# The opening of a two-block transformer on one core: modulation rows by column tiles, mean square by token, two lru chunks worked in pairs of blocks

## The reference, cut to what matters

```python
mod = (c @ w_ada + b_ada)[:, None, :]            # c: 1 x 1024, w_ada: 1024 x 6144
sh_m, sc_m, g_m, sh_f, sc_f, g_f = jnp.split(mod, 6, axis=-1)
h = rms_norm(x) * (1 + sc_m) + sh_m              # x: 512 tokens x 1024
proj = h @ w_in
x_lru, q_down, kv_down, k_rope, gate_a, gate_b = jnp.split(proj, IN_SPLIT_POINTS, axis=-1)
y_a = rg_lru(causal_depthwise_conv(x_lru, conv_w, conv_b), positions, ...)
```

## Time and profile before

| | before |
|---|---|
| median of three runs | 3159.71 us |
| the profiled execution's own time | 3160.7 us |
| its span | 3159.0 us |
| TensorE (PE) busy | 2889.7 us, 91% |
| VectorE (DVE) busy | 1243.8 us, 39% |
| ScalarE (ACT) busy | 748.3 us, 24% |
| mean granted TensorE clock | 0.957 |

### The profile page before, as it was taken

The page is one execution under the profiler, slowest core; times in us unless marked ns, Lnnn a source line. Parts: engine busy times, 40 slices in busy tenths (PEclk is TensorE's granted clock), DMA queues, the critical chain, the costliest instruction groups (busy, mean ns, idle before and its releaser), DMA issues.

```text
span 3159.0 us, 36442 instructions
## 1 busy us (share of the span) xinstructions
PE 2889.7 (91%) x13284; PEld 1776.6 (56%) x13284; DVE 1243.8 (39%) x2119; ACT 748.3 (24%) x1068; POOL 111.2 (4%) x171
## 2 busy tenths in 40 slices
PE   6997899999999899999998979999998999998984
PEld 5775578887778667788776763333332333332221
DVE  6883656765484454334266531111111111111113
ACT  3633432122373334222232320000000000000001
POOL 0020000000000000000010000000000000000001
PEclk7999999999999999999988979999999999999997
DMA  7264136664314022242322059594699979979995
GB/s 234 80 215 132 56 109 183 193 190 124 107 56 118 14 67 67 78 116 77 90 68 85 14 200 383 202 380 150 239 408 410 395 304 408 410 301 410 410 410 197
DMA packets 392991, 638.66 MB, mean 202 GB/s; under 512 B 28400, under 2 KB 278384, under 8 KB 392896
## 3 DMA queue, kind: packets, MB, share of 16 engines
q1 hardware_dynamic: 374784, 590.76, 52.3%
q0 software_dynamic: 9376, 31.14, 2.8%
q10 hardware_dynamic: 8736, 15.47, 1.4%
HBM read 610.77 MB, written 26.54 MB: 202 GB/s over the span
## 4 chain that ended last, share of the span: by engine, by line
PE 72%; DVE 7%; SPq 7%; DMA 7%; ACT 5%; issue 2%; POOL 0%; ACTq 0%; DVEq 0%; another core or an unknown queue 0%
PE bank L2274 24%; PE bank L189 13%; PE bank L191 12%; PE bank L190 12%; SPq L2164 5%; DMA ring<-w_down 4%; DMA ring<-w_gate 2%; PE bank L196 1%; PE bank L2279 1%; PE bank L899 1%; PE bank L900 1%; SPq L295 1%; PE bank L2266 1%; PE bank L940 1%; DVE WLO L162 1%
## 5 line engine op out<-in xcount | busy, mean ns | idle before, releaser
L2274 PE MATMUL bank<-ring,xT 128*64 128x512 f32 x3200 | 717.7, 595 | 43.8 <-DMA ring<-w_gate 21.6
L189 PE MATMUL bank<-HH,WHI 128*128 128x512 f32 x1360 | 551.5, 406 | 34.4 <-DVE HL L573 24.8
L190 PE MATMUL bank<-HL,WHI 128*128 128x512 f32 x1360 | 534.9, 393 | 0.0
L191 PE MATMUL bank<-HH,WLO 128*128 128x512 f32 x1360 | 534.5, 393 | 0.0
L2274 PEld LDWEIGHTS bank<-ring,xT 128*64 128x64 f32 x3200 | 220.1, 137 | 490.9 <-issue 384.6
L2274 PE MATMUL bank<-ring,hT 128*64 128x512 f32 x1600 | 360.0, 595 | 27.5 <-DMA ring<-w_down 25.8
L162 DVE TENSOR_TENSOR WLO<-RAW,WHI 128x2048 fp32r<-128x2048 f32 (+1 forms) x133 | 283.1, 2128 | 134.5 <-ACT WHI L154 134.4
L189 PEld LDWEIGHTS bank<-HH,WHI 128*128 128x128 f32 x1360 | 258.5, 190 | 108.4 <-DVE HL L573 20.4
L154 ACT ACTIVATE WHI<-RAW 128x2048 fp32r<-128x2048 f32 (+1 forms) x133 | 236.6, 1779 | 238.3 <-PE bank L191 177.5
L190 PEld LDWEIGHTS bank<-HL,WHI 128*128 128x128 f32 x1360 | 259.6, 191 | 54.0 <-issue 3.7
L191 PEld LDWEIGHTS bank<-HH,WLO 128*128 128x128 f32 x1360 | 258.8, 190 | 55.2
(11 more groups left out here) (397 smaller groups left out, 2920.5 us busy)
## 6 DMA issues: line engine op xcount, KB each, us to landing
ring<-w_gate SPq DMA_DIRECT2D x128, 1024.0 KB, 11.7
ring<-w_up SPq DMA_DIRECT2D x128, 1024.0 KB, 14.3
ring<-w_down SPq DMA_DIRECT2D x128, 1024.0 KB, 15.9
RAW<-w_ffn_in SPq DMA_DIRECT2D x88, 512.0 KB, 5.2
RAW<-w_ada SPq DMA_DIRECT2D x40, 1024.0 KB, 5.3
RAW<-w_in SPq DMA_DIRECT2D x37, 1024.0 KB, 5.6
RAW<-w_ffn_out SPq DMA_DIRECT2D x32, 704.0 KB, 4.7
expert_results<-ysb ACTq DMA_DIRECT2D x102, 128.0 KB, 5.5
```

Of the source, the lines that this page charges most:

```text
L189: pe.matmul(out, lhi, rhi, start=start, stop=False)
L190: pe.matmul(out, lhi, rlo, start=False, stop=False)
L191: return pe.matmul(out, llo, rhi, start=False, stop=stop)
L2274: ins = pe.matmul(out[halves(h), :], xT[:, k % 4, halves(k // 4)], m["ring"][:, c, at:at + 512], start=False, stop=k == KD - 1)
```

## The change

Loads: positions go before x, x comes in four parts by token tile, and mask comes last. The eight w_ada pieces go into four slots `pairs`; a pair p is column piece p (shift) and piece p + 4 (scale), and is loaded among the w_in chunks: pair 0, w_in 0 and 1, pairs 1 to 3, w_in 2 and 3. Pair 2 waits for rows(0), pair 3 for rows(1), the lru gate weights for rows(3).

Mean square: ScalarE squares each token tile of x as loaded, with an accumulator (one number per token), takes the root of 128x4; VectorE's reciprocal is of 128x4; TensorE spreads it with `root(0)`. The Sin moves behind the last HH.

Modulation: `rows(p)` multiplies with c, repeated 32 times, as the stationary operand and the weights as the moving one, 16 matmuls of 256 columns, in four tiles of 32 columns of the array; VectorE copies the rows to acc, `turned(p)` turns and adds them into columns of bank 6 (4 matmuls). Blocks 2p and 2p + 1 can then be normalized. `first_products(p)` does those two blocks for both first lru chunks (four banks). gates(0) stands between the halves of lru 2, gates(1) after it.

```diff
 def layer_loads(sp, L, m, W):
+    def pair(p):
+        if p >= 2:
+            sp.wait_ge(*sg.event("rows", p - 2))
+        for c in range(2):
+            i = p + 4 * c
+            sp.dma_start(m["pairs"][:, 2 * (p % 2) + c, :].rearrange("p (k n) -> p k n", k=KD),
+                         w_ada[:, :, i * 256:(i + 1) * 256]).then_inc(*sg.inc(f"pair_in{p}", also=[("pair", p)], n=16))
...
+        if not L.prev and n in PAIRS_BEFORE:
+            for p in PAIRS_BEFORE[n]:
+                pair(p)
...
-                sp.wait_ge(*start.event("ada_done"))
+                sp.wait_ge(*sg.event("rows", 3))
@@ layer_act
+    def opening():
+        for k in range(KD):
+            if k % 2 == 0:
+                act.wait_ge(*sg.event("pair_out", k // 2))
+            act.wait_ge(*sg.event("dve_h", ("n", 0, k)))
+            if k >= 2:
+                act.wait_ge(*sg.event("hl", (0, k - 2)))
...
+            act.activation(m["nh"][:, k % 2, :], source, ACT.Identity, **h)
+            act.activation(HH[:, k, :], source, ACT.Identity, **h).then_inc(*sg.inc("act_hi", ("h", 0, k)))
+            if k == 1:
+                feed(1)
+        act.wait_ge(*start.event("st_ang"))
+        act.activation(m["T"][:], m["ang"][:], ACT.Sin)
@@ layer_dve, opening()
+        scaled(0)
+        for p in range(4):
+            c = 2 * p
+            v.wait_ge(*sg.event("rows", p))
...
+            v.tensor_copy(m["acc"][:, p % 2, :], b[5 if p % 2 else 7][:, 0:256]).then_inc(*sg.inc("dve_out", ("rows_sb", p), also=[("rows_sb", p)]))
+            v.wait_ge(*sg.event("pair_col", p))
+            v.tensor_tensor(mod[:, c:c + 2], b[6][:, c:c + 2], vec[:, V_BADA + c:V_BADA + c + 2], ALU.add)
...
+            if p < 3:
+                scaled(p + 1)
+            if p == 0:
+                feed(1)
+            rest(p)
@@ layer_pe
+    def rows(p):
+        pe.wait_ge(*sg.event("pair", p))
...
+        for k in range(KD):
+            for c in range(2):
+                q = 32 * (2 * c + k % 2)
+                ins = pe.matmul(out[q:q + 32, 0:256], m["c"][:, k:k + 1].broadcast_to([P, 32]),
+                                m["pairs"][:, 2 * (p % 2) + c, k * 256:(k + 1) * 256], start=k < 2, stop=k >= KD - 2)
...
+    def first_products(p):
+        for g in range(4):
+            hi, lo = weights(g // 2)
...
+            for k in (2 * p, 2 * p + 1):
...
+                ins = split3(pe, b[g][:], hi[:, c:c + P], lo[:, c:c + P], HH[:, k, :], HL[:, k, :], k == 0, k == KD - 1)
...
+        pe.wait_ge(*start.event("st_eva", 4))
+        root(0)
...
+        rows(0)
+        turned(0)
+        for p in range(4):
+            if p < 3:
+                rows(p + 1)
+                turned(p + 1)
+            first_products(p)
+        dense("lru", 2, between=lambda: gates(0))
+        gates(1)
+        dense("lru", 3)
+        gates(2)
@@ start_program
-        engine.dma_start(m["x0"][:], W["x"][0].rearrange("(t p) d -> p t d", p=P)).then_inc(*sg.inc("st_x", n=16))
+        for t in range(NT):
+            sp.dma_start(m["x0"][:, t, :], W["x"][0, t * P:(t + 1) * P, :]).then_inc(*sg.inc(f"st_x{t}", n=16))
...
-            engine.activation(m["sq"][:, k % 2, :], m["X"][:, k, :], ACT.Square).then_inc(*sg.inc("st_sq", k))
+            act.activation(m["sq"][:].rearrange("p a n -> p (a n)"), m["x0"][:, t, :], ACT.Square, accum_out=m["rc"][:, t:t + 1]).then_inc(*sg.inc("st_sq"))
```

More of the change, by code:

```diff
@@ L328, in norm @@
     def norm(t, eps):
[L330 to L337, removed]
+        act.wait_ge(*(sg.event("stat", t) if t else L.prev.sg.event("stat", 2)))
+        act.activation(m["rc"][:], b[4][:, 0:NT], ACT.Sqrt, bias=K[:, eps:eps + 1], scale=1.0 / D).then_inc(*sg.inc("act_root", t))
         scale, shift = (8, 0) if t == 0 else (32, 24)
@@ L555, in norm @@
         v.wait_ge(*sg.event("act_root", t))
[L556 to L563, removed]
+        root = b[4]
+        v.reciprocal(m["rc"][:], m["rc"][:]).then_inc(*sg.inc("dve_out", ("rc", t), also=[("rc", t)]))
+        v.wait_ge(*sg.event("spread", t))
         for k in range(KD + 1):
@@ L581, in layer_dve @@
         modulate(b[6], 0, 48, ("ada_out", 0), ("ada_out", 1))
+        norm(0)
     else:
-        v.wait_ge(*start.event("ada_done"))
-        modulate(b[6], 0, 16, ("ada_out", 0))
-    norm(0)
+        opening()
     sm, hb = m["sm"], m["hb"]
@@ L829, in dense @@
         for j in range(2):
+            if j and between:
+                between()
             out = bank(g + j)
@@ L851, in layer_pe @@
     if L.prev:
         root(0)
[L853 to L856, removed]
+        for i in range(4):
+            dense("lru", i, norm=None if i else 0)
+            if i:
+                gates(i - 1)
+    else:
+        pe.wait_ge(*start.event("st_eva", 4))
+        root(0)
+        pe.wait_ge(*start.event("st_c"))
+        pe.wait_ge(*start.event("st_eva", 6))
+        rows(0)
[9 more added lines that the diff above has]
+        gates(2)
@@ L966, in layer_pe @@
     stat(2, (KD - 2, KD - 1))
[L969 to L970 removed]
+START_SIGNALS = "st_x0 st_x1 st_x2 st_x3 st_k st_mask st_c st_pos st_dve st_xt st_ev st_eva st_sq st_root st_ang"
 def start_program(engine, who, sg, m, b, W):
@@ L1075 @@
+    if who == "pe":
+        pe = engine
+        pe.wait_ge(*sg.event("st_k"))
+        for t in range(NT):
+            pe.wait_ge(*sg.event(f"st_x{t}"))
+            for k in (4, 1, 0, 3, 2, 5, 6, 7):
+                ins = pe.transpose(b[k][:, t * P:(t + 1) * P], m["x0"][:, t, k * P:(k + 1) * P], K[:, K_ID:K_ID + P])
+                if t == NT - 1:
+                    ins.then_inc(*sg.inc("st_xt", k))
 TWO_PI = (6.28125, 0.0019350051879882812, 3.019915981956753e-07)
@@ L1240, in _ @@
         def _(pe):
-            phases_of(pe, "pe", lambda e, L, after: layer_pe(e, L, m, b), lambda e, n: moe_pe(e, moe, m, b, n))
+            phases_of(pe, "pe", lambda e, L, after: layer_pe(e, L, start, m, b), lambda e, n: moe_pe(e, moe, m, b, n))
         @block.gpsimd
```

165 lines of the change are left out of this document (81 added, 84 removed).

## The result

The changed kernel takes **3144.15 us** (median of 7 runs, 3138.20 to 3145.52) and the kernel before 3161.39 us (7 runs, 3153.96 to 3164.47). The ratio is 0.995, with a 95% interval of 0.9939 to 0.9960: 17.2 us faster by the medians. The forecast was 3146 us. The profiled execution of after has 3138.2 us, span 3136.4, and is the fastest of its seven; the one of before had 3160.7 and 3159.0.

The account below looks back on a forecast made before the run. The opening's chain through TensorE's statistics and matrix-vector products, then the lru tails, was taken to bound the kernel. T0 13.8 us earlier gave 3146.9 from 3160.7, less 1.0 above the median: 3146 us, range 3138 to 3157.

Parts of the forecast that it names:

- T0: Start of the first lru tail on ScalarE, after gates(0); forecast 82.6 us, 13.8 earlier than 96.40, the end moving equally.
- Pair cost, 2.3 us: Sixteen modulation matmuls of a pair on four 32-wide column tiles: 2.3 us at full clock, 4.5 at half.
- rows(0) 4.5 and turned(0) at half clock: First modulation pair on TensorE at half clock: rows(0) from 18.5 to 23.0, copy and turned(0) to 25.4 us.
- Products start at 38.6: First products on TensorE start at 38.6 us instead of 63.0, after VectorE's WLO, HL and copy for pair 1.
- Clock: TensorE's clock in the first product phase: 4 us at half, making it 38.6 to 45.9; other three phases 5.5 each.
- Sin not hidden, 1.9 us: Sin moved ahead of ScalarE's exp load adds 1.28 us table load and 0.6, since VectorE's log1p waits for exp.
- xc sets this and not TensorE: VectorE's xc steps end at 79.1 and set T0; TensorE waits 2.8 us for WLO 2, losing that gain.
- Rival 1: Column tiles share only in part: a pair 3.9 us at full clock, T0 86.7 to 88.6, 3150 to 3153; chance 0.15.
- Rival 2: Column tiles do not overlap: a pair 7.2 or 14.4 us, T0 about 102, 3166 us, nothing gained; chance 0.10.
- Rival 4: TensorE's clock stays at half through the four product phases, 10.3 us each: T0 110.7, 3174 us; chance 0.05.
- Rival 3: A just-covered link between 82.6 and 267 us becomes the wait, such as TensorE's clock: 3152 to 3158; chance 0.08.
- Rival 5: All better: full clock from 18.5 us and pairs of 1.8 us, T0 75.5, 3139 us; chance 0.07.

Follow-up runs that it names:

- e1: Changed kernel with the 16 matmuls of a modulation pair issued one column tile after the other; 3151.56 us, ratio to before 0.9973.
- e4: Changed kernel with the load of positions moved back behind x; 3148.76 us, ratio to before 0.9968.
- e10: Changed kernel without column tiles, c repeated 128 times, rows copied in two parts, half the turning matmuls gone; 3158.44 us, ratio to before 1.0013.
- e2: Changed kernel with gates(0) after all of lru 2 instead of between its halves; 3146.81 us, ratio to before 0.9955.
- e5: Changed kernel with all four modulation pairs, rows and turns, on TensorE before any first product; 3142.46 us, ratio to before 0.9943.
- e11: e6 plus five 128x512 matmuls of unused result behind turned(0); 3139.94 us, ratio to before 0.9948.
- e0_again: The changed kernel measured a second time without edit; 3143.99 us, ratio to before 0.9952.
- e6: Changed kernel with Sin, exp, log and the lru constants moved ahead of and inside the opening; 3139.33 us, ratio to before 0.9931.
- e3: Changed kernel with the Sin right behind feed(1) on ScalarE instead of behind the last HH; 3140.69 us, ratio to before 0.9941.
- e9: Changed kernel with two column tiles of 64, c repeated 64 times, neighbouring matmuls on different tiles; 3146.21 us, one run.
- e8: Changed kernel with two column tiles of 64, c repeated 64 times, issued tile by tile; 3156.33 us, one run.
- e7: Changed kernel with a pair's matmuls alternating between only two of the four column tiles at a time; 3142.69 us, ratio to before 0.9948.

## Why the prediction was right, point by point

- **The end moves with T0.** Shown. The distance from T0 to the load of the second layer's vectors is 687.4 us in before and 686.4 to 690.3 in the thirteen other profiles, while T0 moves from 74.4 to 96.4; from T0 to the end of the span it is 3058.6 to 3066.1. Each version with T0 clearly later (e1, e4, e10) is slower by its median too. Shifts of T0 of some 5 us and less don't show one for one in the medians (e2, e5, e11).
- **Pair cost, 2.3 us.** The term was a little too high: 1.93, near the ideal end of 1.8. The reading of two-tile overlap from the 64-wide row held. What decides is that the next matmul has another column tile (4.59 in line). The rule of the Trainium skill, TensorE: Matmul & The Clock Gate, Part 3 (a load overlaps matmuls in flight only if its row group differs), doesn't agree with these traces: all loads use all rows, and in e10 loads are busy for 5.89 of the 7.07 us of a pair while matmuls are busy for all of it, in one and the same tile.
- **rows(0) 4.5 and turned(0) at half clock.** Mis-sized: 2.38 and 1.05 in after, 3.21 and 1.05 in e0_again. The clock was already up during rows(0). pair 0 landed as computed, 18.5.
- **Products start at 38.6.** They started at 35.11 (36.88 in e0_again). Pair 1 landed at 30.4 (30.5). The forecast then waited for VectorE (two WLO, two HL, until 36.3) ahead of the copy for pair 1. In after this was not the last link: VectorE was done at 33.25, 3.0 early because rows(0) and turned(0) were short, and waited 0.46 us for rows(1), so the chain ran through the landing of pair 1 and rows(1). In e0_again the two were even (VectorE done at 34.69, rows(1) at 34.61). turned(1) at full clock gave the rest in after. But as a way to the gain this step carried little: e5 gives it up and loses nothing by its median.
- **Clock.** 4 us at half in products(0) were assumed: e0_again and e6 show over 5, after none. The assumption lies between them, and that executions of one program differ here by 2.7 us in T0 was not foreseen.
- **Sin not hidden, 1.9 us.** Shown by e3. From the last HH to the end of hb the sum gave 8.2 us (62.8 to 71.0), and after has 8.2 (56.55 to 64.79).
- **"xc sets this and not TensorE."** Just true in e0_again, where xc ends at 76.96 and gates(0) starts at 76.95. Wrong in after: there xc was ready at 72.63 and TensorE at 74.21. The step that failed there is the time of half a chunk behind the wait: 5.5 forecast, 7.17 measured with the clock down. The wait itself was forecast at 2.8 and measured at 2.72 and 2.73.
- **T0 82.6.** 77.84 in the fastest execution of after and 80.58 in the slowest of e0_again. From the last HH to T0 the sum gave 19.8 us; e0_again has 19.7 and after 21.3 (1.5 of them the clock). What was too high stands ahead of the last HH: rows(2) was put at 45.9 and started at 40.73 in after and 45.06 in e0_again, and a later pair with its copy and turn was put at 4.0 and took 3.4. That the forecast of 3146 met the median of 3144.15 so closely has a part of luck: it was set from the median of three runs, 3159.71, and seven gave 3161.39. The gain itself was put at 13.8 and came out at 17.2, and at 15.6 in e0_again's batch.
- **Nothing lost behind T0.** Up to the start of the w_uq loads this holds exactly (123.2 to 123.3 us from T0 in before, after and e0_again). The 1.9 us behind them in after are 0.3 in e0_again.
- **Rival 1** (a pair 3.9 us) can be tested by e9, 3.67 us: T0 81.49, earlier than the 86.7 given, and its single time 10.0 below its before, about what the rival gives (7 to 10). **Rival 2** was priced by 7.2 us for tiles that don't overlap at all. Only e10, without tiles, comes to that (7.07), and there its conclusion "nothing is gained" holds; 32-wide tiles in line still overlap where the tile changes, 4.59 (3151.56). **Rival 4** didn't occur: through rows and turns the clock is 1.00 in after from 35 to 65 and in e0_again from 45. **Rival 3**: no link behind T0 took the gain away. Half clocks of 1.6 to 1.7 us do occur behind the wait for WLO 2 and in the statistics matmuls (under e2), in some executions and not in others. **Rival 5** (all better, T0 75.5) came nearest to the profile of after: pairs of 1.93 and full clock from the first product on, 77.84, with 1.6 of the difference from the clock behind WLO 2. By the median, 3144.15 against its 3139, it didn't occur.

## What to carry to other kernels

A matrix-vector product on TensorE whose weights have to be streamed anyway was cheapest here with the weights as moving operand, the vector repeated only as wide as one narrow column tile, and successive matmuls in different tiles: 1.93 us instead of 7.07 for the same products, and without it the rest of the change brought nothing. The order of issue is a part of the recipe: tile by tile, the same narrow matmuls take 4.59. When work is pulled forward, look for what it then waits on: here it was ScalarE's table loads and VectorE's constants in front of the next weight chunk, and with these moved (e3, e6) the medians are 3.5 and 4.8 us lower again, at the edge of what these runs can tell. Compare medians of several executions before a difference of a few microseconds in two profiles is explained: the same program gave profiles 10.3 us apart.

## What the runs showed of the hardware that was not expected

- In one column tile a record of 256 moving columns takes as long for 128, 64 and 32 stationary columns: four records in 1.03 to 1.05 us at full clock (e10, e8, e1). Other tiles run beside it: eight records with two tiles in turn (e9), sixteen with four (after).
- Where a row of matmuls goes over from one tile to the next, records of both run side by side for a while, seven in 1.08 us (e8). So even tile by tile a pair costs 6.31 us with one such change and 4.59 with three, instead of 7.07 with none. The forecast had no term for that.
- The wait of TensorE for WLO 2, 2.7 us long, dropped the granted clock to half in four profiles (after, e1, e2, e9) and left it at full in five (e0_again, e4, e7, e8, e10). It costs 1.6 us where it falls. What decides was not found.
- At the first products the clock was full from the start (after) or half for over 5 us (e0_again), in two executions of one program. Five filler matmuls (e11) held it up until the next wait, of 2.27 us, and no longer.
